# ScalarE empties the first bank of a down unit at that unit's own place in its order, ahead of the selection tick that follows

## What is computed

```python
score = einsum('bqhl,bqh->bql', relu(s), wi)               # indexer score of every earlier key
_, idx = lax.top_k(score, topk)                            # 256 keys for each query
a_o = sparse_attend(q, take(k, idx), take(v, idx), valid)  # 8 heads, 2 key/value heads
s_o = glu_out(s5_scan(u, h0, h0, *ssm_w)[0], w_glu, b_glu, dtype)
mix = concatenate([a_o, s_o], -1) @ w_out
x = x + rmsnorm(mix, g_post)
hdn = square(relu(rmsnorm(x, g_ffn_pre) @ w_up))           # 1024 -> 4096
y = x + rmsnorm(hdn @ w_down, g_ffn_post)                  # 4096 -> 1024
```

## Time and profile before

| | |
|---|---|
| median of 3 runs | 3634.23 us (3627.4 to 3640.02) |
| profiled execution | 3627.5 us, of which 3625.8 us are its span |
| TensorE busy | 3036.5 us, 84% of the span |
| VectorE busy | 1840.4 us, 51% |
| ScalarE busy | 1637.7 us, 45% |
| GpSimd busy | 1262.6 us, 35% |
| mean granted TensorE clock | 0.915 of full speed |

### The profile page before, as it was taken

How to read it: one execution, slowest core, us unless ns; L and a number is a source line. 1 busy time by engine, 2 the same in 40 slices (tenths; PEclk the granted TensorE clock), 3 DMA queues, 4 the chain that set the end, 5 groups by cost and what they waited for, 6 DMA issues and landing times.

```text
span 3625.8 us, 46903 instructions
## 1 busy us (share of the span) xinstructions
PE 3036.5 (84%) x15347; PEld 2396.8 (66%) x15352; DVE 1840.4 (51%) x4116; ACT 1637.7 (45%) x2873; POOL 1262.6 (35%) x1181
## 2 busy tenths in 40 slices
PE   7998545546678889997799999968989999699997
PEld 5887431224556668764577886645778888588885
DVE  4433872862357884468686332666782333511112
ACT  3322413612447755575463555745634554322222
POOL 1333621324013561153265113522672112224444
PEclk9999777877879999998899999988999999899999
DMA  4444344636336564354454223343444213544443
GB/s 149 142 146 142 93 126 133 170 118 202 111 123 232 206 244 134 115 200 154 157 193 169 79 85 124 126 171 122 177 159 136 73 62 131 191 147 150 174 151 125
DMA packets 216109, 529.45 MB, mean 146 GB/s; under 512 B 57514, under 2 KB 110828, under 8 KB 189852
## 3 DMA queue, kind: packets, MB, share of 16 engines
q1 hardware_dynamic: 202924, 501.94, 40.6%
q0 software_dynamic: 11360, 22.60, 2.0%
q10 hardware_dynamic: 1584, 1.90, 0.2%
HBM read 399.43 MB, written 134.12 MB: 147 GB/s over the span
## 4 chain that ended last, share of the span: by engine, by line
PE 50%; DVE 11%; issue 9%; ACT 5%; DMA 4%; POOL 4%; SPq 2%; ACTq 0%; POOLq 0%; DVEq 0%
PE r L1620 16%; PE r L1657 12%; PE po L1708 6%; PE tr L1699 3%; ACT junk_a_b L1982 2%; PE sc L1686 2%; PE sc L1687 2%; POOL acc_b L2124 1%; PE sc L1676 1%; DVE junk_v_b L2363 1%; PE r L1817 1%; POOL hr_b L2105 1%; DVE trial_b L2315 1%; PE tr L1676 1%; PE r L1586 1%
## 5 line engine op out<-in xcount | busy, mean ns | idle before, releaser
L2124 POOL TENSOR_TENSOR acc_b<-acc_b,part_b 128x512 f32<-128x512 f32 x375 | 516.2, 1398 | 483.0 <-ACT part_b L1933 482.1
L1657 PE MATMUL r<-ready_b,h_b 128*128 128x512 f32 x2304 | 574.4, 403 | 41.5 <-ACT part_b L1933 38.3
L1657 PEld LDWEIGHTS r<-ready_b,h_b 128*128 128x128 f32 x2304 | 434.2, 193 | 155.5 <-ACT part_b L1933 51.1
L1620 PE MATMUL r<-x_hi_b,ready_b 128*128 128x512 f32 x1536 | 516.5, 400 | 5.4 <-DVE x_lo_b L2229 2.8
L2105 POOL TENSOR_TENSOR hr_b<-hr_b 128x512 f32<-128x512 f32 x128 | 149.0, 1164 | 766.7 <-ACT hr_b L1920 766.5
L1982 ACT ACTIVATE junk_a_b<-score_b,trial_b 128x384 int8<-128x384 f32 (+13 forms) x266 | 347.4, 1306 | 100.8 <-DVE trial_b L2315 99.7
L1620 PEld LDWEIGHTS r<-x_hi_b,ready_b 128*128 128x128 f32 x1536 | 291.3, 190 | 72.2 <-issue 10.1
L1933 ACT ACTIVATE part_b<-r 128x512 f32<-128x512 f32 x390 | 223.9, 595 | 220.5 <-PE r L1657 131.8
L1708 PEld LDWEIGHTS po<-V_sb,pT_b 128*128 128x128 f32 x2176 | 286.7, 191 | 23.4 <-ACT pT_b L2009 4.5
L1620 PE MATMUL r<-x_lo_b,ready_b 128*128 128x512 f32 x768 | 301.6, 393 | 0.0
L1708 PE MATMUL po<-V_sb,pT_b 128*128 128x64 f32 x2176 | 279.2, 268 | 3.7 <-DVE o_b L2380 3.3
(11 more groups left out here) (407 smaller groups left out, 6061.1 us busy)
## 6 DMA issues: line engine op xcount, KB each, us to landing
ready_b<-ws_u SPq DMA_DIRECT2D x96, 1024.0 KB, 6.6
ready_b<-ws_d SPq DMA_DIRECT2D x96, 1024.0 KB, 5.0
ws_u<-up_b SPq DMA_DIRECT2D x32, 1024.0 KB, 8.7
ws_d<-dn_b SPq DMA_DIRECT2D x30, 1024.0 KB, 6.4
kv_b<-kv_pages POOLq DMA_DIRECT2D x128, 128.0 KB, 3.5
kv_b<-kv_pages SPq DMA_DIRECT2D x128, 128.0 KB, 3.1
raw_b<-w_out SPq DMA_DIRECT2D x64, 256.0 KB, 3.2
raw_b<-w_up SPq DMA_DIRECT2D x32, 512.0 KB, 5.4
```

The lines of the kernel that those rows point to most:

```text
L1620: mm = pe.matmul(x[:], wt[:, c], y[:, k], start=k == n == 0, stop=(k, n) == (KD - 1, 2))
L1657: mm = pe.matmul(x[:], f[:, tok], w[:, col], start=c == n == 0, stop=(c, n) == (KQ - 1, 2))
L2124: pool.tensor_tensor(dst, dst, part[:, add_no[key] % 2, :], ALU.add).then_inc(add_pool, 1)
```

## The change

`behind` no longer empties both banks of the down unit before; it empties only its second bank. The first bank's copy is a function of its own, `empty_sum`, which ScalarE calls at the end of the down unit's own place: after the second bank of the unit before, the splits and the features of this place, and ahead of the tick that follows in the plan. Banks that VectorE empties are left as they are. Waits, operands and the order among the copies do not change; the same semaphore counts the freed banks.

```diff
--- before.py
+++ after.py
@@ -1894,6 +1894,18 @@
                     act.wait_ge(mean_ok, mean_no[x])
                     act.activation(root[:, z], mean[:, z], ACT.Sqrt).then_inc(root_ok, 1)
 
+                def empty_sum(key):
+                    if sum_by[key] != "act":
+                        return
+                    _, g, m, h, i = key
+                    act.wait_ge(ring_full, full_at(key))
+                    if m == 0:
+                        dst = acc(i)[:, 512 * h:512 * h + 512]
+                    else:
+                        dst = part[:, add_no[key] % 2, :]
+                        wait(act, add_pool, add_no[key] - 2)
+                    act.activation(dst, ring[bank_no[key] % RING][:], ACT.Copy).then_inc(free_act, 1)
+
                 def behind(u):
                     if u is None:
                         return
@@ -1920,17 +1932,8 @@
                             act.activation(s, x, ACT.Relu).then_inc(free_act, 1)
                     elif kind == "D":
                         g, m, r = u[1:]
-                        for h, i in down_banks(g)[2 * r:2 * r + 2]:
-                            key = ("D", g, m, h, i)
-                            if sum_by[key] != "act":
-                                continue
-                            act.wait_ge(ring_full, full_at(key))
-                            if m == 0:
-                                dst = acc(i)[:, 512 * h:512 * h + 512]
-                            else:
-                                dst = part[:, add_no[key] % 2, :]
-                                wait(act, add_pool, add_no[key] - 2)
-                            act.activation(dst, ring[bank_no[key] % RING][:], ACT.Copy).then_inc(free_act, 1)
+                        for h, i in down_banks(g)[2 * r + 1:2 * r + 2]:
+                            empty_sum(("D", g, m, h, i))
                     elif kind == "F":
                         for h in range(2):
                             act.wait_ge(ring_full, full_at((*u, h)))
@@ -1973,6 +1976,9 @@
                         square_sum(u)
                     elif kind in "ME" and u[3] in (2, 7):
                         square_root(u)
+                    elif kind == "D":
+                        h, i = down_banks(g)[2 * u[3]]
+                        empty_sum(("D", g, u[2], h, i))
 
                 def count_upper(t, i):
                     n = turn_s[t]
```

## The result

The changed kernel takes 3610.6 us (median of 7, 3602.7 to 3618.0) against 3633.4 us of the kernel before (median of 7, 3623.9 to 3640.0), ratio 0.9943, 95% interval 0.9927 to 0.9959. Two later comparisons gave 0.9933 (0.9921 to 0.9946) and 0.9934 (0.9921 to 0.9947). By the means of all 17 executions against 56 of before, pooled over these and the comparisons with the experiments, it is 21.4 us faster (18.9 to 23.9). Forecast were 24 us and 3610.

The account below looks back on a forecast made before the run. TensorE was taken as the bound, waiting 68.2 us for ScalarE's down bank copies, late in order, not work. Terms 22 + 3 + 4 + 2 - 3 - 4 = 24 us gave 3610 us, range 3587 to 3638.

Parts of the forecast that it names:

- The entries: 21 TensorE waits in front of the fourth bank of a down group: 22 us gained, bounds 17 and 27.5.
- the later waits: Four TensorE waits later in a down group, 6.4 us together: half gained, 3 us (0 to 6.4).
- the clock: Shorter TensorE waits keep some of its granted clock from dropping: 2 us gained (0 to 8).
- VectorE's stretch: 1100 to 1300 us, VectorE 86% busy, weight splits among its work: half of six places' gain lost, -3 us.
- The ends: Two feed group ends beside a search: one add and one copy leave the chain, 4 us gained (0 to 18).
- Downstream: Counts behind moved copies start up to 0.6 us later and VectorE waits for them: -4 us (0 to 13).
- A: Rival, chance 0.20: delayed counts make the search loop take the gain back, leaving 9 or about 5 us.
- Its second part: Small VectorE trial instructions meet earlier GpSimd adds on a shared port: 23 us lost if all did, on the path.
- B: Rival, chance 0.10: more than forecast, all upper bounds together 60 us, 18 of them at feed group ends.
- C: Rival, chance 0.08: ScalarE blocks on banks TensorE fills late in later units, 38 us lost, 14 us slower.

Follow-up runs that it names:

- e1: Changed kernel, but only the first bank of each group's first down unit is copied at its own place; ratio 0.9963 to the kernel before, 3616.7 us.
- e2: Changed kernel, but only first banks of the later units are moved, the first unit's staying as before the change; ratio 1.0008 to the kernel before.
- e10: Changed kernel with a rule by stretch: both banks, only the first unit's first bank, or none moved; ratio 0.9931 to the kernel before, median 3606.3 us.
- e11: The same rule by stretch as e10 run again, beside the changed kernel on one chip; ratio 0.9928 to the kernel before, median 3603.3 us.
- e4: The kernel before, unchanged, traced a second time to see how far two traces of one kernel drift apart; 3626.5 us.
- e3: Changed kernel, but without the move in the last slice of each feed group; ratio 0.994 to the kernel before, 3611.0 us.
- e8: Changed kernel plus a 0.6 us ScalarE pause behind each group's moved first bank; ratio 0.9959 to the kernel before, 7.2 us above the changed kernel.
- e7: Changed kernel, but both banks of every down unit beside the search are copied at the unit's own place; ratio 0.993 to the kernel before.

## Why the prediction was right

- **The entries, 22 us, with the later waits 3, the clock 2 and VectorE's stretch -3.** These were 24 us in five stretches; three traces give 23.6, 23.1 and 24.3. The mechanism, a wait one bank later and shorter by about a bank, stands in the rows of 1238.73. e1 gained 18.2 in these stretches and e2 2.2: the first unit is most of it, not all. But the sum hit because two of its terms were off in opposite ways, as the point on the clock shows.
- **VectorE's stretch.** I took off 3 of 6.6 us there and it gained 6.7. The three traces in which only the first unit's copy is moved there (e1, e10, e11) gained 8.8, 8.8 and 7.5, e2 lost 2.1: a loss exists, about 2 us, and it comes from the later units. That it is VectorE's splits was not tested.
- **The clock, +2.** This term was too small, and the 22 for the entries too large by nearly as much. The stretch 0:0-9 and the sum of the five stretches, before and after (length, TensorE's busy time and matmuls; the granted clock is third from the end):

```profile
1101.96:1478.52 376.56, 333.36 (x1620) 0.95 0.56 197
...
sum 877.40, PE 799.88; mean PE 159.98
```

```profile
1106.17:1475.70 369.53, 330.73 (x1621) 0.97 0.57 201
...
sum 853.79, PE 794.39; mean PE 158.88
```

Of the 23.6 us gained, 5.5 are TensorE's busy time, for the same matmuls, and 18.1 its idle time. The other two traces of the changed kernel give 7.4 and 15.6, and 8.2 and 16.0; in e4 the busy time is that of before to 0.2 us. Forecast were 2 of clock and 22 of waits (22 + 3 - 3). The clock came back in three of the five slices with a wait of 2 us or longer: in 0:1, 1:12 and 2:2 the granted clock was 0.90, 0.94 and 0.88 and is 1.00. At the place of the earlier trace rows, slice 0:4, nothing came back: behind the 2.41 us wait 24 matmuls took 7.33 us, 1.6 more than at the rate before, as after the 4.23 us wait. The granted clock over a window behind it (PEclk third from the end):

```profile
1241.00:1246.00 5.00, 5.00 (x18) 3.96 (x18) 4.72 (x13) 3.58 (x6) 4.40 (x5) 0.76 0.31 128
```

- **The ends, +4.** This step failed: it is 0 (e3: 0.4 and 0.6). I counted what leaves the chain of copy, add and norm, and did not look at what the last copy itself stands behind, a root that waits for VectorE.
- **Downstream, -4.** It came as -5, but not by the path that I had given (a count 0.6 us later), so the size agrees by luck. 0.9 us are lost in 1:4-9, and 4.1 in slices 8 and 9 of group 2, where the search ends. There the feed meets VectorE's scan of the scores. Before (first TensorE, then VectorE's scan, GpSimd's square, its adds):

```profile
2703.00 4.24 PE L1657 MATMUL r<-ready_b,h_b 128*128 128x512 f32 x18
2703.03 4.42 DVE L2347 TENSOR_TENSOR_SCAN score_b<-tie_b 128x2048 f32<-128x2048 bf16 x1
...
2703.88 4.41 POOL L2105 TENSOR_TENSOR hr_b<-hr_b 128x512 f32<-128x512 f32 x1 [1.97 <-ACT hr_b L1920]
...
2711.53 3.31 POOL L2124 TENSOR_TENSOR acc_b<-acc_b,part_b 128x512 f32<-128x512 f32 x1
```

After:

```profile
2681.43 6.96 PE L1657 MATMUL r<-ready_b,h_b 128*128 128x512 f32 x30
...
2682.30 1.15 POOL L2111 TENSOR_TENSOR hr_b<-hr_b 128x512 f32<-128x512 f32 x1 [2.36 <-ACT hr_b L1932]
...
2684.20 1.49 POOL L2119 TENSOR_TENSOR h_b<-hr_b,h_b 128x512 fp32r<-128x512 f32 x1 [0.74 <-ACT h_b L1952]
2684.57 5.40 DVE L2353 TENSOR_TENSOR_SCAN score_b<-tie_b 128x2048 f32<-128x2048 bf16 x1
2685.64 11.94 POOL L2130 TENSOR_TENSOR acc_b<-acc_b,part_b 128x512 f32<-128x512 f32 x3
...
2691.11 0.60 ACT L1907 ACTIVATE part_b<-r 128x512 f32<-128x512 f32 x1 [6.02 <-POOL acc_b L2130]
...
2691.76 2.93 PE L1657 MATMUL r<-ready_b,h_b 128*128 128x512 f32 x6 [3.37 <-ACT part_b L1907]
```

Before, the scan delayed a square (4.41 us, after the change 1.15), and the adds ran behind it. After, the first add meets the scan: ScalarE's next copy waits 6.02 us for the buffer, three adds take 11.94 us, and TensorE waits 3.37. All variants lose here, even e2, which is slower elsewhere, and e10 and e11, which leave the copies of this stretch where they were (4.4 and 2.5 us): it is not the copies moved inside this stretch that cost. That the adds' meeting with the scan is the cause is read from these rows and not tested. By the Trainium skill, "SBUF — State Buffer" (SBUF: two separate sides), a VectorE instruction with two inputs in SBUF and a GpSimd instruction that reads SBUF exclude each other for a whole instruction; the scan reads its flags as both of its inputs. The rows agree: the copy that needs the add begun at 2685.64 starts at 2691.11, about an add's length (1.29 us at its median) behind the scan's end at 2689.97.
- **Rivals.** A (search takes it back) is the right picture for a part: e8 puts its price at 40% of a delay, not at all of it. Its second part, small VectorE instructions held up by more adds, is small at most: VectorE was busy 2.7 us longer in the whole span (1840.4 to 1843.1). B failed with the ends. C is refuted by e7.
- So the total is right in part by luck. The errors cancelled: too much for the waits against too little for the clock, +4 for the ends that were nothing against -3 in VectorE's stretch that was nothing either. What the stretches of the ledger lack (18.4) to the 21.4 us measured lies in stretches where one trace cannot tell.

## What to carry to other kernels

Where an engine in order empties a ring for another, look for the one bank of a group that the ring's length makes the hostage, and move that copy alone ahead of foreign work: here 37 of the 147 moved copies, 27 of them ahead of counts, brought about two thirds of the gain. The sum of waits is a poor forecast (of 68 us 57 were left with e1, which gained 14.7 us in the executions, and 34 with the change, which gained 21.4); the distance by which the next needed bank comes later is the better one. A shorter wait can also give back clock, here a quarter to a third of what the entries gained, so compare TensorE's busy time for the same matmuls and not its waits alone. And a gain inside a stage is only worth what the next stage's other inputs allow, so follow each input of its first instruction back before counting it.

## What the runs showed of the hardware

- Two traces of one kernel agree to 0.1 us over hundreds of microseconds and part in a few steps of 1 to 5 us, the largest inside the ledger at slice 10 of group 0 with the granted clock (0.91 to 1.00 there). So a ledger between points of the program reads effects of 1 us in stretches where the traces of one kernel agree, where whole executions scatter by 16.
- A GpSimd add took 1.29 us at its median and 5.38 beside VectorE's scan (count, min/median/max ns in the changed kernel):

```profile
L2130 POOL TENSOR_TENSOR acc_b<-acc_b,part_b x375: 1255/1292/5377, 1145.4 to 3583.4; 128x512 f32<-128x512 f32 x188
```

- The granted clock fell behind some waits of TensorE and not behind others: 24 matmuls took 7.33 us after 2.41 us (above, 0.76), but elsewhere in the changed kernel 5.73 and 5.70 us after shorter waits (1.00 over 1147 to 1152 and over 1208 to 1214):

```profile
1147.11 5.73 PE L1657 MATMUL r<-dn_b,h_b 128*128 128x512 f32 x24 [1.32 <-ACT part_b L1907]
...
1208.90 5.70 PE L1657 MATMUL r<-dn_b,h_b 128*128 128x512 f32 x24 [1.61 <-ACT part_b L1907]
```
